# Second expert pair: two left-over chunks and the scatter products one chunk later, the up bias ahead of the third chunk, the first activation ahead of the adds

## The reference

```python
logits = einsum('td,de->te', h, w_router) + b_router        # 32 experts
top_vals, top_idx = top_k(logits, 4);  gates = softmax(top_vals)
# for every expert e, on the tokens that chose it:
u = xb @ w_up[e] + b_up[e]                                   # 1024 -> 2048
glu = minimum(u[:, 0::2], 7.0);  lin = clip(u[:, 1::2], -7.0, 7.0)
a = glu * sigmoid(1.702 * glu) * (lin + 1)
y = a @ w_down[e] + b_down[e]                                # 1024 -> 1024
# x = x + sum over the four experts of gate * y
```

## Time and profile before

| what | value |
| --- | --- |
| median of the runs | 1150.89 us |
| the profiled execution | 1149.04 us |
| its span, first to last instruction | 1147.1 us |
| TensorE busy | 1094.3 us, 95% |
| VectorE busy | 445.6 us, 39% |
| ScalarE busy | 184.8 us, 16% |
| weights queue, share of 16 DMA engines | 91.3%, 435.83 MB |

### The profile page before, as it was taken

The page is one execution under the profiler, slowest core; times in us unless marked ns, Lnnn a source line. Parts: engine busy times, 40 slices in busy tenths (PEclk is TensorE's granted clock), DMA queues, the critical chain, the costliest instruction groups (busy, mean ns, idle before and its releaser), DMA issues.

```text
span 1147.1 us, 14808 instructions
## 1 busy us (share of the span) xinstructions
PE 1094.3 (95%) x5914; PEld 494.8 (43%) x5943; DVE 445.6 (39%) x882; ACT 184.8 (16%) x394; POOL 88.7 (8%) x161
## 2 busy tenths in 40 slices
PE   9999999999999999999899999999999999999997
PEld 6688899553333333333333333333333333333332
DVE  4867786753343233233223232323232323232322
ACT  2133231211321101010101010101010101010101
POOL 1775115000000000000000000000000000000000
PEclk9999999999999999999999999999999999999999
DMA  9945639999999999999999999999999999999996
GB/s 320 329 135 158 196 92 350 414 359 419 397 419 428 416 432 431 431 431 434 430 431 432 434 431 433 430 431 434 430 433 432 433 432 428 433 434 430 425 424 284
DMA packets 53204, 444.35 MB, mean 387 GB/s; under 512 B 13100, under 2 KB 19372, under 8 KB 35740
## 3 DMA queue, kind: packets, MB, share of 16 engines
q1 hardware_dynamic: 46712, 435.83, 91.3%
q0 software_dynamic: 5600, 7.32, 2.4%
q10 hardware_dynamic: 852, 0.64, 0.2%
HBM read 439.78 MB, written 2.37 MB: 385 GB/s over the span
## 4 chain that ended last, share of the span: by engine, by line
PE 61%; DMA 37%; issue 1%; DVE 1%; ACT 0%; SPq 0%; DVEq 0%
PE pA L2001 31%; PE pB L2001 22%; DMA ring<-in_w_up 21%; DMA ring<-in_w_down 10%; PE pM L2001 6%; DMA area<-in_w_up 5%; PE pM L2004 1%; DMA ring<-in_w_in 1%; PE pA L2004 1%; ACT area L1223 0%; DVE x L1848 0%; SPq L775 0%; DVE conv_row L1762 0%; DVE area L1923 0%; DVE x L1928 0%
## 5 line engine op out<-in xcount | busy, mean ns | idle before, releaser
L2001 PE MATMUL pA<-ring,hn 128*64 128x512 f32 x1536 | 352.6, 602 | 23.2 <-DMA ring<-in_w_up 23.2
L2001 PEld LDWEIGHTS pA<-ring,hn 128*64 128x64 f32 x1536 | 105.3, 137 | 219.1 <-issue 185.5
L2001 PE MATMUL pB<-ring,area 128*64 128x512 f32 (+2 forms) x784 | 171.5, 591 | 6.6 <-DMA ring<-in_w_down 5.8
L2001 PE MATMUL pB<-area,ring 128*128 128x132 f32 (+2 forms) x928 | 140.3, 342 | 0.6 <-DMA ring<-in_w_in 0.6
L2001 PE MATMUL pA<-area,hn 128*64 128x512 f32 x512 | 119.3, 610 | 10.4 <-DMA area<-in_w_up 10.4
L2001 PEld LDWEIGHTS pB<-area,ring 128*128 128x128 f32 (+1 forms) x928 | 115.7, 175 | 22.4 <-issue 3.3
L2001 PEld LDWEIGHTS pB<-ring,area 128*64 128x64 f32 (+2 forms) x784 | 58.5, 136 | 101.2 <-issue 87.8
L1848 DVE TENSOR_TENSOR x<-pM,x 128x512 f32<-128x512 f32 x60 | 40.1, 692 | 147.7 <-PE pM L2001 147.7
L1211 ACT ACTIVATE area<-area 128x512 f32<-128x512 f32 x30 | 18.9, 631 | 385.5 <-DVE area L1831 385.5
L1762 DVE COPY conv_row<-pM 128x512 f32<-128x512 f32 x30 | 20.6, 686 | 146.2 <-PE pM L2001 146.2
L2001 PEld LDWEIGHTS pA<-area,hn 128*64 128x64 f32 x512 | 36.1, 139 | 74.6 <-issue 59.7
(11 more groups left out here) (351 smaller groups left out, 942.5 us busy)
## 6 DMA issues: line engine op xcount, KB each, us to landing
ring<-in_w_up SPq DMA_DIRECT2D x36, 4096.0 KB, 29.8
ring<-in_w_down SPq DMA_DIRECT2D x18, 4096.0 KB, 29.0
area<-in_w_up SPq DMA_DIRECT2D x12, 4096.0 KB, 30.2
ring<-in_w_up SPq DMA_DIRECT2D x16, 2048.0 KB, 12.8
area<-in_w_down SPq DMA_DIRECT2D x6, 4096.0 KB, 30.0
ring<-in_w_in SPq DMA_DIRECT2D x22, 1024.0 KB, 12.2
ring<-in_w_down SPq DMA_DIRECT2D x16, 1024.0 KB, 10.6
ring<-in_w_up SPq DMA_DIRECT2D x16, 1024.0 KB, 8.4
```

The source lines that it names most:

```text
L2001: return pe.matmul(out, w, m, start=start, stop=stop, skip_group_check=True)
```

## The change

On TensorE in pair 1: `up(1)` stands ahead of the first left-over chunk and `up(2)` ahead of the second; `up_biases(0)` stands on its own ahead of `up(2)`, behind the wait for the selection, and `biases(0)`, now with the down bias alone, behind `up(4)`; the four scatter products and the sample's stand behind `up(5)`. On VectorE in pair 1 `activate(0)` stands ahead of the four adds. No instruction is added or removed.

```diff
@@ VectorE, pair @@
+                    if kind == "second":
+                        activate(0)
                     for k in range(4):
                         add(k, *OUTPUTS[k])
-                    activate(0)
+                    if kind != "second":
+                        activate(0)
                     add_sample(4)
@@ TensorE, biases(e) @@
-                    if not (first and e == 0):
+                    if e or not (first or pair1):
                         up_biases(e)
@@ TensorE, pair @@
                     up(0)
                     if pair1:
+                        up(1)
                         left_over(0)
-                        up(1)
+                        pe.wait_ge(sel_ready, g + 1)
+                        up_biases(0)
+                        up(2)
                         left_over(1)
-                        up(2)
-                        biases(0)
                         up(3)
                         up(4, freed=True)
-                        for k in range(4):
-                            scatter(k)
-                        scatter_sample(bank(4))
+                        biases(0)
                     else:
...
                     biases(1)
                     up(5)
-                    if not pair1:
+                    if pair1:
+                        for k in range(4):
+                            scatter(k)
+                        scatter_sample(bank(4))
+                    else:
                         act_turn(0)
                     up(6)
```

## The result

The changed kernel takes 1152.11 us in the median of 22 runs (1150.21 to 1154.79), the kernel before 1149.49 in 22 runs (1147.9 to 1151.41), the three of the first table among them. The ratio is 1.0023, interval 1.0018 to 1.0029: **2.6 us slower** (2.1 to 3.3). The profiled execution took 1153.55 us, with a span of 1151.7, against 1149.04 and 1147.1 before. In the text a cost in us is the ratio less one, times the median before.

A forecast was written before the change was run, and what follows sets the result against it. The weight queue was taken to set the end. Pair 1 on TensorE +1.9 us, of which +1.0 reaches the end, on the median of 1150.89 gave 1151.9 us, range 1149.7 to 1153.9.

The forecast's parts named there:

- TensorE's new order: Pair 1 on TensorE: the same pieces laid end to end, first scatter at 316.0 us, `up(1)` 4 us earlier.
- The chain of VectorE and ScalarE: Pair 1: first add 6.1 us later, at 318.6; TensorE waits 2.1 us at the third scatter, `up(6)` 1.9 us late.
- The gap at 302 us: Weight queue, 302 to 310 us: 329 GB/s against 427, 1.8 us of transfer lost, mostly closed by earlier frees.
- What becomes of the 1.9 us: Weight queue issues at 372.92 and 382.67 us: TensorE's lateness reaches the end as +1.0 us (0 to +1.9).
- the list of signs: Signs to check: TensorE's wait of about 2.1 us, above 400 GB/s at 302 to 310, a dip at 322 to 340 or 380 to 395.
- The queue covers the stall: Rival, weight queue: TensorE waits 2 us but a lead of 2.3 us is enough; 1150.9 us, chance 0.20.
- The landing of 397.3: Sign, transfer issued at 382.67 us: if its landing moves less than 0.4 us, the queue covered the stall.
- No stall, gap closed: Rival, pair 1: adds ready when TensorE comes, gain between -0.4 and -1.8 us; 1149.1 to 1150.5 us, chance 0.13.
- The wait repeats at the gather: Rival, `gather(bank(6), 1)`: late if the third `hn` quarter starts after 323.6 us; up to 1153.8 us, chance 0.17.

The follow-up runs named there:

- a: The change, with VectorE's order left as before (four adds ahead of the first activation); 1151.48 us, ratio 1.0012.
- e: The change, with the first two quarters of `hn` made ahead of reading the left-over chunks' output; 1149.61 us, ratio 1.0003.
- k: The change, with the left-over chunks and the up bias back where they stood before; 1149.63 us, ratio 1.0001.
- l: The change, with the scatters back behind `up(4)` as before; 1156.71 us in 5 runs, ratio 1.0060.
- i: The kernel before, with the last `x` turn of pair 1 written four times on TensorE near 346 us; 1150.83 us, ratio 1.0009.
- b: The kernel before, with only VectorE's order of the change (first activation ahead of the adds); 1152.88 us, ratio 1.0023.
- c: The kernel before, with a group of TensorE transposes written five times in pair 1, 2.1 us more work; 1152.04 us, ratio 1.0020.
- d: The kernel before, with a group of TensorE transposes written five times in pair 2, at 383.5 us; 1150.45 us, ratio 1.0006.
- j: g, with the last `x` turn of pair 1 written four times on TensorE near 346 us; 1150.25 us, ratio 1.0004 against the kernel before.
- g: The kernel before, with weights of pairs 3 and 4 in 2 MB halves, pair 3's first ones issued sooner; 1150.64 us, ratio 1.0009.

## Why the prediction was right, and which term was mis-sized

The forecast was 1151.9 us, in a range of 1149.7 to 1153.9, and 1152.11 was measured. That the two are 0.2 us apart is luck: the forecast's base was the median of 3 runs, 1150.89, and 22 runs of the kernel before give 1149.49. On that base the same sum makes 1150.5. The change is +2.6 us where +1.0 was forecast; a base 1.4 us too high made up for most of a cost 1.6 us too low.

- **TensorE's new order**: right. The scatters were laid at 316.0 and came at 316.24, `up(6)` at 321.35 and came at 321.74, of which 0.35 is older than the pair.
- **The chain of VectorE and ScalarE**: right. First add 318.6 forecast, 318.96 measured; the wait 2.1 forecast, 2.21 measured, at the place named. Experiments a, e, k and l show the cause from four sides: the wait falls at the third scatter with the activation first (change), at the gather with the adds first (a), is gone if the quarters of `hn` don't hang on the left-over chunks (e) or if the second of these is back (k), and grows to 6.3 us if the scatters come one chunk sooner (l). What the prediction took for a rival, the wait at the gather, is the other face of the same late chain.
- **The gap at 302 us**: closed as forecast (420 GB/s). But its size before was read from one execution: in the other kernels in which nothing ahead of 302 us differs from the kernel before, i has 329, k 349, b 361, c 364, d and j 366 and g 374. Against 363, their middle, the gap is 1.2 us (8 x (427 - 363) / 427), not 1.8.
- **What becomes of the 1.9 us**: this is the step that failed, in size and in place. It was set at +1.0, the middle of 0 to 1.9. All of it reaches the end, and the cost is 2.6. The step had it arrive at the issues of 372.92 and 382.67, with a lead of 2.2 us at the second; the lead there was 5.5 us, since the queue was late itself by then. It had lost the time at 318 to 346 us, a place that the step never looked at, though the list of signs behind it allows a dip there. The step also took the lead that suffices for one number. It isn't: in the change 2.9 us lost 3.5 and 2.7 us lost nothing, and in a the transfer issued at 334.64, with 2.1 us ahead of it, landed 2.7 us behind the one before, 0.2 us lost:

```profile
ring<-in_w_up SPq DMA_DIRECT2D x1, 1024.0 KB, 4.8
```

- **The queue covers the stall** (chance 0.20): out. The landing of 397.3 was to move less than 0.4 us, and moved 3.1. The Trainium skill, "DMA: Bandwidth & Descriptors", anatomy of one DMA, gives a fixed part of about 2.0 us, fitted on the GpSimd path; by it the stall would be covered. The quickest 1 MB transfer cited here, 4.8 us in a, comes near to it with 2.4 us beside the moving (1 MB at 430 GB/s, 2.4 us); the one at 329.50 took 8.9 us, of which 2.9 were for the one ahead and 3.5 were lost. The delay was not covered, and the measurement decides.
- **No stall, gap closed**: the stall came. Experiment e, which is this case made on purpose, gives +0.3 us (-0.7 to 1.4), not -0.4 to -1.8.
- **The wait repeats at the gather**: it didn't; the third quarter started at 323.46, 0.14 us ahead of the point named. Experiment a shows that rival's mechanism at 1.87 us.

Six kernels side by side. TensorE's lateness is taken from the start of pair 1 to its first down chunk, against 44.6 us before; the landing is that of the transfer that was issued at 336.15 us and landed at 344.3 before:

| kernel | TensorE late, us | GB/s, 302 to 318 | GB/s, 318 to 346 | landing late, us | cost, us (interval) |
|---|---|---|---|---|---|
| before | 0 | 378 | 419 | 0 | 0 |
| k, left-over chunks back | 0.0 | 386 | 419 | 0.4 | +0.1 (-0.9 to 1.1) |
| e, no stall, gap closed | -0.1 | 417 | 403 | -0.3 | +0.3 (-0.7 to 1.4) |
| a, adds first | 2.0 | 418 | 384 | 1.1 | +1.4 (0.3 to 2.4) |
| c, delay alone | 2.1 | 395 | 387 | 1.9 | +2.3 (1.3 to 3.3) |
| b, stall alone, clock fell | 3.7 | 390 | 353 | 4.7 | +2.6 (1.6 to 3.7) |
| the change | 2.0 | 421 | 373 | 4.2 | +2.6 (2.1 to 3.3) |

The stretches end at 346 us because b loses most ahead of 322 us (212 GB/s from 318 to 322). The kernels in which TensorE is late in pair 1 lose transfer from 318 to 346 us and cost 1.4 to 2.6 us; the two in which it is not cost nothing that can be measured. Beyond that the columns don't agree in size: b and the change land 4.2 to 4.7 us late in their traces and cost 2.6 in the medians. What the closed gap gives back can't be told from c and a (both 2 us late; a has the gap closed and costs 0.9 us less, within the intervals), nor from b. In e it is 0.7 us at the most, and is not shown to be more than nothing.

Open: the change costs 2.6 us (2.1 at the least) where TensorE is 2.0 us late. Whether the rest is a loss on the queue beyond the lateness was not settled; the 3.5 us at the issue of 329.50 speaks for it, in one execution, and a, as late on TensorE, has no such row. So is why b, with 3.7 us of lateness, costs no more, and why shorter, earlier transfers in pairs 3 and 4 give nothing. None of the versions is faster than the kernel before; k and e are as fast.

## What to carry to other kernels

Where the transfers are issued when a busy engine has read what lay there, closing a gap in the queue may give nothing if the issues behind it come no sooner: here most of the gap moved behind them, and no gain could be measured (e). Before moving a chunk ahead of another, follow its output: here the moved chunk's readers fed a chain of four quarters that two later TensorE steps needed, and the order on VectorE could only choose which of the two would wait (a and the change). And look for the next wait behind a stall before removing it: a took the stall away and met one of 1.87 us at the gather. For the worth of a stall, look at the first issues behind it, not at the tightest-looking transfer of the whole stage.

## What was not expected of the hardware

- How much work must be left ahead when a 1 MB transfer is issued varied within and between traces: in the change 2.9 us lost 3.5 and 2.7 us lost nothing; in a 2.1 us lost 0.2; in the kernel before 4.8 us lost nothing. In c a delay of 1.9 us passed straight through to the landing. No single lead can be read from them.
- Idle times of TensorE and the granted clock behind them: 2.21 us in the change and 1.87 us in a left it at 1.00. 2.42 us in b was followed by 0.50 (1.2 GHz) from 317 to 320 us, and from the third scatter to `up(6)` it was 7.61 us where the kernel before takes 6.16; 6.30 us in l by 0.50 from 320 to 324 us, and 18 matmuls took 3.50 us for 2.12. So the stalls of b and the change, 0.2 us apart in length, made TensorE late by amounts 1.7 us apart (3.7 and 2.0).
- GB/s of an 8 us stretch differs between kernels that are the same up to there: 329 to 374 from 302 to 310 us in eight kernels. A loss of under 1 us read from one such row is not to be trusted.
